# A fused two-block transformer kernel: a reordered attention stage, two thirds of the modulation moved behind the expert gather, and the attention's output weights loaded into the upper halves of the weight slots

## The reference, cut to what matters

```python
# first block
h = rms_norm(x, attn_norm_g)
q, k, v, qi, ki, wi, glu_in, gates = split(h @ w_in)         # 512,512,512,512,64,8,1024,2048 columns
y_att = dsa_attention(rms(q), rms(k), v, qi, ki, wi, rel_bias) @ w_att_out
#   two blocks of 128 queries: index scores relu(qi.ki)*wi, the 64 best keys, softmax with a bias
y_conv = silu(layer_norm(conv31(a * sigmoid(g)))) @ w_conv_out
x = x + (g0 * y_att + g1 * y_conv) @ w_out
x = x + peer(rms_norm(x))            # 128 experts of each token are gathered: rows of 2 x 1024 floats
x = x + sigmoid(rms_norm(x) @ w_ple_gate) * (p @ w_ple_proj)
# second block
mod = silu(c) @ ada_w + ada_b        # 6 x 1024 numbers: sh1, sc1, g1, sh2, sc2, g2; sh1, sc1 for c_ctx too
x = x + g1 * mixer_block(rms_norm(x) * (1 + sc1) + sh1, states from the context)
x = x + g2 * conv_ffn(rms_norm(x) * (1 + sc2) + sh2)
out = rms_norm(x)
```

## Time and profile before

| | |
|---|---|
| median of 3 runs | 1561.48 us (1560.96 to 1563.71) |
| span of the profiled execution | 1554.9 us; the page gives no other time for it, so 6.6 us of the median lie outside this span or between executions |
| busy: PE, DVE, ACT, POOL | 1212.9, 926.5, 431.5, 347.1 us |
| the chain that ended last | PE 58%, DMA 22%, DVE 10%, ACT 4%, issue 3%, POOL 2% |
| moved by DMA | 409.73 MB, of which the gather's queue and the modulation (POOL's) 297.35 MB |

### The profile page before, as it was taken

The page is one execution under the profiler, slowest core; times in us unless marked ns, Lnnn a source line. Parts: engine busy times, 40 slices in busy tenths (PEclk is TensorE's granted clock), DMA queues, the critical chain, the costliest instruction groups (busy, mean ns, idle before and its releaser), DMA issues.

```text
span 1554.9 us, 26679 instructions
## 1 busy us (share of the span) xinstructions
PE 1212.9 (78%) x11282; PEld 834.9 (54%) x11282; DVE 926.5 (60%) x2067; ACT 431.5 (28%) x1094; POOL 347.1 (22%) x315
## 2 busy tenths in 40 slices
PE   7989898894385533457856775799987888999998
PEld 6467784772153100125524452468877774888843
DVE  2887666657797988785677655321455343455512
ACT  2111420132432422543364332423243211110100
POOL 1000012034354555454455544000000000000000
PEclk9997999996597855569878996899999999999999
DMA  9551459699999999999999999624300023344432
GB/s 381 195 191 66 144 205 390 238 383 419 414 410 420 420 422 421 421 414 419 416 421 420 420 418 418 240 82 163 109 9 3 4 111 108 122 163 161 137 140 104
DMA packets 109720, 409.73 MB, mean 264 GB/s; under 512 B 8456, under 2 KB 33552, under 8 KB 76448
## 3 DMA queue, kind: packets, MB, share of 16 engines
q0 software_dynamic: 44576, 297.35, 46.5%
q1 hardware_dynamic: 63552, 106.48, 19.2%
q10 hardware_dynamic: 1472, 4.20, 1.0%
HBM read 405.89 MB, written 2.11 MB: 262 GB/s over the span
## 4 chain that ended last, share of the span: by engine, by line
PE 58%; DMA 22%; DVE 10%; ACT 4%; issue 3%; POOL 2%; another core or an unknown queue 0%; POOLq 0%; DVEq 0%; ACTq 0%; SPq 0%
PE psum L502 20%; DMA arena<-in_experts,arena 17%; PE psum L1942 8%; PE psum L2454 5%; PE psum L512 4%; DVE arena L1490 4%; PE psum L1521 3%; DMA arena<-in_lora_up 2%; PE psum L755 2%; PE psum L1269 2%; POOL arena L1475 2%; PE psum L2244 2%; PE psum L760 2%; DMA arena<-in_ada_wT 2%; PE psum L741 2%
## 5 line engine op out<-in xcount | busy, mean ns | idle before, releaser
L1475 POOL DMA_INDIRECT arena<-in_experts,arena x256 | 317.1, 1239 | 383.2 <-PE psum L1521 299.8
L1521 PE MATMUL psum<-arena 128*32 128x512 f32 x1024 | 185.4, 805 | 238.2 <-ACT arena L1506 231.6
L502 PE MATMUL psum<-actT,weights 128*128 128x256 f32 x1312 | 287.3, 381 | 0.0
L502 PEld LDWEIGHTS psum<-actT,weights 128*128 128x128 f32 x1312 | 250.3, 191 | 35.7 <-issue 1.5
L1521 PEld LDWEIGHTS psum<-arena 128*32 128x32 f32 x1024 | 22.7, 121 | 329.5 <-ACT arena L1506 307.3
L1490 DVE CUSTOM_DVE_ANT_0 arena<-arena 128x1024 f32<-128x1024 f32 x96 | 116.7, 1224 | 50.9 <-DMA arena<-in_experts,arena 50.1
L1490 DVE CUSTOM_DVE_ANT_0 arena<-weights,arena 128x1024 f32<-128x1024 f32 x96 | 116.6, 1223 | 37.1 <-DMA arena<-in_experts,arena 35.1
L1496 ACT ACTIVATE arena<-arena 128x2 f32<-128x2 f32 x128 | 26.1, 204 | 364.3 <-DVE arena L1490 350.4
L1942 PE MATMUL psum<-arena 64*64 64x64 f32 (+1 forms) x2816 | 89.7, 231 | 17.4 <-DVE arena L2059 7.1
L1942 PEld LDWEIGHTS psum<-arena 64*64 64x64 f32 x2816 | 84.1, 142 | 26.0 <-issue 14.6
L1490 DVE CUSTOM_DVE_ANT_0 arena<-normed,arena 128x1024 f32<-128x1024 f32 x64 | 77.2, 1225 | 22.1 <-DMA arena<-in_experts,arena 20.3
(11 more groups left out here) (390 smaller groups left out, 1897.0 us busy)
## 6 DMA issues: line engine op xcount, KB each, us to landing
weights<-in_w_in SPq DMA_DIRECT2D x18, 2048.0 KB
arena<-in_ada_wT POOLq DMA_DIRECT2D x48, 512.0 KB, 6.3
weights<-in_ffn_w_up SPq DMA_DIRECT2D x22, 1024.0 KB
weights<-in_ffn_w_down SPq DMA_DIRECT2D x5, 2048.0 KB
weights<-in_w_out SPq DMA_DIRECT2D x4, 2048.0 KB
weights<-in_w_peer_q SPq DMA_DIRECT2D x4, 2048.0 KB
arena<-in_experts,arena POOLq DMA_INDIRECT x256
weights<-in_w_ple_gate SPq DMA_DIRECT2D x2, 2048.0 KB
```

The costliest lines, as they stand in the source:

```text
L502: mm = nc.tensor.matmul(out[:, c * T:(c + 1) * T], w[:, k, c * P:(c + 1) * P], act[:, k, :], start=(k == 0), stop=(k == kc - 1))
L1475: nc.gpsimd.indirect_dma_start(out=rows[:, n % RING, :], out_offset=None, in_=dram["experts"], in_offset=bass.IndirectOffsetOnAxis(ap=eidx ...
L1521: mm = nc.tensor.matmul(SUMS[sum_part(k, i), i, :], diag[:, pos, :], rows[:, pos, D + 512 * i:D + 512 * (i + 1)], start=first, stop=last, ...
```

## The change

Four parts. (a) The mirrored bias table moves forward, behind `glu_a`, on PE and ACT. (b) PE's order in the attention stage: products of gate and output tiles are cut into chunks of 16 matmuls and set between the steps that wait on DVE and ACT; both `conv_out` tiles go into the second query block's waits. `some(10)` becomes `some(2)` ahead of q's and k's root and `some(8)` behind their scaling. (c) `att_out0/1` are loaded into the upper halves of the slots, behind the tiles used four places before, with a landing semaphore of their own. (d) Only modulation blocks 0 to 15 are computed before the gather. POOL loads the other 32 after the gather's last row has been used, along with `c` again; ACT takes its SiLU after n3's chunks; DVE runs these 32 dots in the embedding's stage and in `dve_x_in`: 8, 6, then 3 at each of five steps, then 2 and 2. The gates g1 and g2 are spread over the partitions by a PE transpose in the chain stage and three DMAs through DRAM on ACT's queue.

```diff
@@ sp_weights, pe_tile
-                    sp.wait_ge(S("tile_done"), i - WSLOTS + 1)
+                    sp.wait_ge(S("tile_done"), i - (2 * WSLOTS if name in UPPER_HALF else WSLOTS) + 1)
+                    first = upper_half(name)                     # 2048 for att_out0, att_out1
+                    dst = ring[:, i % WSLOTS, first:first + kc * width]...
@@ pe_project (moved here from the head of pe_attention)
             pe_features(pe, "glu_a", actT)
+            pe.wait_ge(S("rel_in"), 64)
+            for i in range(4):
+                mm = nc.tensor.matmul(aux[i], K("flip"), toepf[:, 512 * i:512 * (i + 1)], start=True, stop=True)
+            mm.then_inc(S("toep_pe"), 1)
@@ pe_attention
             mm.then_inc(S("qk_t"), 1)
+            gate0 = pe_features_by_chunk(pe, "gate0", actT)
+            next(gate0)
             pe.wait_ge(S("qT_cp"), 1)
...
                 if b:
+                    next(gate0)
                     pe.wait_ge(S("ix_relu"), b)
                 index_or_logits(b, qiT, ...)
-            pe_features(pe, "gate0", actT)
+            all_of(gate0)
...
             pe_features(pe, "gate1", actT)
+            gate2 = pe_features_by_chunk(pe, "gate2", actT)
+            next(gate2)
             pe.wait_ge(S("cv_dve"), 2)
...
+            next(gate2)
             pe.wait_ge(S("cv_rt"), 1)
+            index_or_logits(0, qT, ..., "lg_pe")
+            all_of(gate2)
+            gate3 = pe_features_by_chunk(pe, "gate3", actT)
+            next(gate3)
+            pe_turn_logits(pe, 0)
+            next(gate3)
+            pe_attend(pe, 0)
+            pe.wait_ge(S("av_cp"), 1)
+            index_or_logits(1, qT, ..., "lg_pe")
+            all_of(gate3)
+            pe.wait_ge(S("cvT_ok"), CC)
+            pe_features(pe, "conv_out0", cvT)
+            pe_turn_logits(pe, 1)
+            conv_out1 = pe_features_by_chunk(pe, "conv_out1", cvT)
+            next(conv_out1)
+            next(conv_out1)
+            pe_attend(pe, 1)
+            all_of(conv_out1)
@@ dve_first
-            some(10)
+            some(2)
             dve.wait_ge(S("qk_rt"), 1)
...
             nc.vector.tensor_tensor(qk4, qk4, bc(qks, P, 4 * AH, HD), ALU.mult).then_inc(S("qk_n"), 1)
+            some(8)
@@ pool
-            for j in range(6 * DC):
+            pool_modulation(pool, range(2 * DC), adaw)
+        def pool_late(pool):                                     # after pool_rows
+            pool.wait_ge(S("row_used"), TB * NSEL)
+            pool.dma_start(late_c, dram["cc"][0:D].partition_broadcast(P)).then_inc(S("c_in"), 16)
+            pool_modulation(pool, range(2 * DC, 6 * DC), late_w)
@@ dve_ple, after n3's chunks
+            late["mod"] = dve_late_modulation(dve, st)
+            late_dots(8)
@@ dve_x_in
             copy_chunks(dve, "n4", gain, shift, 1)
+            late_dots(6)
...
-            all_of(dve_scan_common(dve, st, x_m, "x"))
+            for _ in dve_scan_common(dve, st, x_m, "x"):
+                late_dots(3)
...
             for _ in range(3):
                 next(direction)
+                late_dots(2)
@@ pe_chain_x
+            pe.wait_ge(S("mod_ok"), 2)
+            nc.tensor.transpose(AUX[0:4 * DC, 0, 0:P], modT[:, 2 * DC:6 * DC, 0], K("ident")).then_inc(S("gates_turned"), 1)
@@ act_gates (new, beside pe_chain_x)
+            nc.scalar.copy(late_c[0:4 * DC, 0:P], AUX[0:4 * DC, 0, 0:P]).then_inc(S("gates_turned"), 1)
+            for g, row in enumerate((0, 3 * DC)):
+                act.dma_start(gate_vec[g].rearrange("(c p) -> c p", p=P), late_c[row:row + DC, 0:P])...
+            act.wait_ge(S("gate_io"), 32)
+            act.dma_start(gatebc..., gate_vec....partition_broadcast(P)).then_inc(S("gate_io"), 16)
```

More of the change, by code:

```diff
@@ L456, in bc, with upper_half, landed @@
             return ap.to_broadcast(list(shape))
-        n_parts = [0, 0]
+        UPPER_HALF = ("att_out0", "att_out1")
+        def upper_half(name):
+            return 2048 if name in UPPER_HALF else 0
+        def landed(i):
+            return S("landed_upper" if upper_half(tiles[i][0]) else f"landed{i % WSLOTS}")
+        n_parts = {}
         landed_at = []
-        for i, (_, _, parts) in enumerate(tiles):
-            n_parts[i % WSLOTS] += len(parts)
-            landed_at.append(16 * n_parts[i % WSLOTS])
+        for i, (name, _, parts) in enumerate(tiles):
+            at = upper_half(name) or i % WSLOTS
+            n_parts[at] = n_parts.get(at, 0) + len(parts)
+            landed_at.append(16 * (len(UPPER_HALF) if upper_half(name) else n_parts[at]))
         def sp_weights(sp):
@@ new lines, in pe_attention, with pe_turn_logits @@
+            pe_turn_logits(pe, 1)
[4 more added lines that the diff above has]
+            all_of(conv_out1)
+        def pe_turn_logits(pe, b):
+            n = b + 1
+            pe.wait_ge(S("lg_n"), b + 1)
+            for s_ in range(AH):
+                for st in range(n):
+                    i = s_ * n + st
+                    mm = nc.tensor.transpose(AUX[:, i // 4, (i % 4) * P:(i % 4 + 1) * P],
+                                             logit[:, s_, st * P:(st + 1) * P], K("ident"))
+            mm.then_inc(S("pt_pe"), 1)
@@ L868, in build, with pe_attend @@
+        def pe_attend(pe, b):
+            n = b + 1
+            pe.wait_ge(S("pt_cp"), b + 1)
+            for s_ in range(AH):
+                ps_, q = part_of(s_)
+                h = HEAD[s_]
+                for st in range(n):
+                    mm = nc.tensor.matmul(AUX[ps_, 0, q * P:(q + 1) * P], vtok[:, st, h * HD:(h + 1) * HD],
+                                          prT[:, s_ * n + st, :], start=(st == 0), stop=(st == n - 1))
+            mm.then_inc(S("av_pe"), 1)
         logit = relu.rearrange("p (s t) -> p s t", s=AH)
@@ L1348, in dve_queries @@
                 pass
[L1349 removed]
+            dve.wait_ge(S("ada_used"), 2 * DC)
             st.settle()
[L1351 to L1359 removed]
+            dve_scales(dve, st, slice(0, 2 * DC), 2, ("x1", "ctx"))
             st.run(nc.vector.tensor_scalar(onemka, C("k_a", 0, RC), -1.0, 1.0, ALU.mult, ALU.add))
@@ L1622, in act_ple_proj @@
                 yield
-            for g in range(2):
-                act.wait_ge(S("gatebc_pe"), g + 1)
-                nc.scalar.copy(gatebc[:, g, :], gate_bank(g)).then_inc(S("gatebc_ok"), 1)
-                yield
         def pe_ple_proj(pe):
@@ L2033, in act_pair @@
             sv_.wait("dve", pair, "M")
+            if full and pair == 0:
+                act.wait_ge(S("ada_used"), 6 * DC)
             nc.scalar.copy(by_chunks(m.N, d, j), heads_of(PS[:, 0:2, :], 256)).then_inc(sv_.sem("act"), 1)
@@ L2282, in act_x_in, with late_dots @@
             act_load(act, "gup", gup, dram["g_up"])
+        late = {}
+        def late_dots(n):
+            for _ in range(n):
+                next(late["mod"], None)
         def dve_x_in(dve, st):
```

143 lines of the change are left out of this document (67 added, 76 removed).

## The result

The changed kernel takes 1539.17 us (median of 4 runs, 1535.85 to 1542.62); the kernel before took 1561.22 us beside it (4 runs). The ratio is 0.9868, 95% interval 0.985 to 0.9886. The forecast of 1538.5 us and its range hold the time, but the way there is not the forecast's, as the trace shows.

The account below looks back on a forecast made before the run. Bound: a chain of waits through DVE ahead of the gather, DMA bytes during it, PE later. Terms -26.4 + 3.5 = -22.9 us on span 1554.9 give 1532.0; plus 6.6 is 1538.6, rounded to 1538.5; range 1532 to 1548.

Parts of the forecast that it names:

- The sum: Whole kernel: 26.4 us saved ahead of the gather, 3.5 us late cost, net -22.9 us on the profiled span.
- signs of being right: Transposes at about 109.4 us, under 2 us; index products 1.7 and 3.0; gather 667 us as before; n3 about 26 earlier.
- Bias table (a) and attention order (b): PE in the attention stage: idle time falls from 15.2 to 3.1 us, saving 12.1; gate0's wait is 2.4.
- The clock: Attention stage: PE operations lengthened by the low clock return to normal, saving 7.7 us (bounds 0 and 7.7).
- A gap here is paid twice: PE in the attention stage: after the 6.3 us gap the same operations also take longer, at granted clock 0.73.
- Mix (c, d): Around the mix product: 1.1 us saved in the gap ahead, 1.6 in the pair of tiles, 3.9 behind it.
- The gather: From 318 to 985 us, set by DMA bytes: keeps its length and moves as a block with its start.
- the rivals on this side: Clock stays low after the projections: 1546 us, chance 0.14; gather does not follow its start: 1558 to 1565, chance 0.02.
- Late modulation (d): Behind the gather: row traffic costs 1.0 us at ple_gate0 and 2.5 at x_v, 3.5 in all.
- late loads slow the weights: Rival behind the gather: both stalls at upper bounds and the clock lowered, late cost 10 us, total 1545; chance 0.15.
- half of the engines for `x_v`'s load: Skill's rule at x_v: queues alternate by packet, so its weights land 4 to 5 us late; total 1541 or more.
- The gates: Gate transpose and three DMAs moved to the chain stage: cost 0, up to 3 us if the DMAs are slow.

Follow-up runs that it names:

- the repeat: The changed kernel run once more without an edit: 1540.77 us, ratio 0.9894 to the kernel before.
- e1: Changed kernel with none of the 32 late rows loaded; the dots still run, without waiting for rows: 1526.61 us, ratio 0.9801 to the kernel before.
- e3: Changed kernel with the first late row held back until ple_gate0's weights have landed: 1538.97 us, ratio 0.9885 to the kernel before.
- e4: Changed kernel with the bias table's transposes back behind the key product (part a undone): 1549.18 us, ratio 0.9961 to the kernel before.
- e8: Changed kernel with PE's old order in the attention (part b undone): 1552.53 us, ratio 0.9968 to the kernel before.
- e6: Kernel before with only the late rows, their dots and the gate rows moved behind the gather: 1559.62 us, ratio 1.0009.
- e7: Changed kernel with all 48 modulation rows and the gates back where they were: 1537.82 us, ratio 0.986 to the kernel before.
- e5: Changed kernel with 4 late dots behind n4 instead of 6, then 0, 0, 0, 8, 6 in the scan's five steps: 1532.32 us, ratio 0.9826.
- e9: Changed kernel with att_out0/1 in ordinary weight slots instead of the upper halves: 1537.72 us, ratio 0.9874 to the kernel before.
- e10: e5 with PE's small gate-row matmuls put back between the gather's last products, their results unused: 1532.51 us, ratio 0.9843 to the kernel before.
- e2: Changed kernel with 0, 0, 0, 6, 6 late dots in the scan's five steps instead of 3 each: 1535.92 us, ratio 0.987.
- e11: e5 run once more without an edit: 1530.65 us, ratio 0.9843 to the kernel before.

## Why the prediction came out right

The time was right by luck, because errors cancelled. The sum was -22.9 us on the span; the profiled spans differ by 16.0, 6.9 less. I then added 6.6 us as time outside the span. In every execution with a profile here the time outside the span is 1.8 us (1540.73 and 1538.9); the rest of the 6.6 was the distance of one execution from its kernel's median, which is a scatter, and the changed kernel's median stands only 0.3 us above its profiled span. That error is 6.3 us the other way. In the repeat's profiled execution, 22.2 us below the one before, the errors cancel inside the sum instead: 30.45 us are saved ahead of the gather and 8.2 lost behind it.

The prediction had named as a sign of being wrong "more than 6 us lost between the end of the gather and the first solve". From n3's norm to the solves the changed kernel lost 12.1 us (163.12 against 151.07) and its repeat 5.9. Of its signs of being right, the transposes came at about the time given, but took 3.24 us and not under 2; the index products and the length of the gather were as said; and n3 came 29.2 us earlier, where it gave about 26.

*Bias table (a) and attention order (b).* The idle time came out better: 0.7 us left where I had 3.1, since PE hardly waited for gate0 (at most the 0.5 us by which its first chunk, 4.01 us, exceeds 3.5). The slow transposes hid part of this wait: in e1's and e3's executions they took 1.94 us, and PE then waited 1.66 and 1.60. The transposes start at 108.17 us, 1.2 earlier than I had, as four bias products now run at 42.78 us where part of their time was free. The clock saved about 6 of the 7.7 us: transposes 3.24 and not 1.97. That I added the parts is what e4 and e8 correct. With the late rows in place, the first row comes at 309.74 us without a and b, 302.89 with a, 302.75 with b, and 287.91 with both: 6.9 and 7.0 us alone, 21.8 together. (The new places of `some(2)` and `some(8)` stay in both e4 and e8; they were not tried by themselves.) Single executions of the changed kernel's front differ, 293.4 us in e1 and e3 where nothing in it was edited, so the size is better read from the ratios: 1.0009 without both, 0.9968 and 0.9961 with one, 0.9868 and 0.9894 with both. That is 6.4 and 7.5 us alone and 18 to 22 together. The clock from 112 to 150 us goes with it: 0.78 without both (e6), 0.81 and 0.82 with one, 1.00 with both. But not every pause lowers it: e1, e3 and e7 waited 1.66, 1.60 and 0.90 us ahead of gate0 and kept 1.00, while e5 waited 0.94 and had 0.94. "A gap here is paid twice" was the right sentence, and the sum should have been made for the two as one.

*Mix (c, d).* Pause ahead 2.72 us (2.6 forecast), the pair 27.73 (27.8), from its end to n2's norm 249.10 - 247.08 = 2.0 us (2.6). All three right in this execution (the last section has others); the upper halves have no share in it (e9).

*The gather* is no shorter: 678.08 us from first row to n3 against 676.94. It moved as a block, and the rivals on this side are out.

*Late modulation (d).* This is the step that failed, "three rows of 0.5 MB at 418 GB/s delay it by 3.8 us, less 1 us of slack: 2.5 us (0 to 5)". Forecast for all of the late cost 3.5 us, measured 14.3 with the tail (7.0 to the solves in the repeat). The kind of cost was right (e1, e5) and the count was wrong. I took the three rows in flight at one moment; but every dot frees a slot and starts the next row, and DVE, idle there, keeps going. From 1016.87 to 1039.21 us twelve rows were issued, seven of them after `x_v`'s load. In the 16 us while `x_v`'s weights came, the queues moved 3.27 MB of rows beside 2.85 MB of weights. (The term has a slip too: 3.8 less 1 is 2.8, not 2.5.) And the stall was paid twice here too: `x_v`'s product ran 1.93 us longer at the low clock, which I had counted only in a rival. That rival (late loads slow the weights, 10 us) was the nearest to what happened.

A second step failed as well. Of DVE's dots with waits for their rows the prediction said that none would stand ahead of a wait of PE. The last of the eight ahead of n4 did, and cost 0.3 us in the changed kernel, 1.1 in its repeat and 1.3 in e9.

The Trainium skill (DMA: Bandwidth & Descriptors, Queues, rings and completion order) says that each DMA engine takes turns between the queues with work, packet by packet. The prediction's estimate from this, half of the engines for `x_v`'s load, was the better guide: the shares of time, 51.6 and 48.1%, agree with it. The estimate of 4 to 5 us lies between the 3.11 and the 7.04 measured. Counted in the packets of the profile, 894 and 1406, the two queues were not even.

*The gates* cost nothing that a run shows at their new place. That taking their matmuls from the gather's end might cost clock at n3 was in no part of the prediction; e10 could not tell such a cost from what executions differ by.

*The best version.* e5: the change with its rows started outside the flight of `x_v`'s weights, 0.9826 and 0.9843 in two sets of runs, against 0.9868 and 0.9894 of the change as made. The ratio of e1, 0.9801, shows what more there would be if the rows were free.

## What to carry to other kernels

When loads are moved into a stretch with idle engines, count how many its consumer will start there, not how many are in flight: a stream over a few slots (four here) with an idle consumer takes its share of the DMA engines as long as it has rows left, and the place of the consumer's instructions is the throttle. Pauses of one engine that lie close together are to be costed as a group, with the clock: removing either of two gave 6 to 8 us, both 18 to 22. And a single profile's distance from the median is no constant to add to a forecast.

## What was not expected of the hardware

The same instructions with the same pause of 2.71 or 2.72 us ahead of them got different clocks from one execution to the next. The 64 matmuls of mix took 27.73 us at a granted clock of 1.00 in the changed kernel, its repeat, e2, e4, e6, e9 and e11, and 30.76 and 30.79 in e1 and e3, where the granted clock was 0.90 over e1's product. e5, e8 and e10 had 29.2 to 29.4. With the slower norm behind it (2.80 instead of 1.83 us) the distance from mix to the gather's first row was 73.24 us in e1 against 68.56, so behind a pause of this length 0 or 4.7 us were lost. What decides it these runs do not show. This is as large as what several parts of the change are worth, and goes some way to explain the spread of up to 13 us between single executions; that it is all of it was not shown.

By bytes the two DMA queues shared about evenly (3.27 and 2.85 MB) though one had packets of 3.7 KB and the other of 2.0 KB (894 and 1406 packets), so that they were not even by these packets.
